# An encoder block with experts: the last iteration of the expert loop written out, and two weight loads moved between row tiles

## What is computed

```python
h = rms_norm(x, norm_mix)
x_in, b_g, c_g, q, k, v, gate_a, gate_b = split(h @ w_in)        # w_in: 1024 x 5120
y_conv = short_conv_mixer(x_in, b_g, c_g, conv_w) @ w_out_conv
y_attn = neighbourhood_attention(rms(q), rms(k), v, rpb) @ w_out_attn
x = x + (sigmoid(gate_a) * y_conv + sigmoid(gate_b) * y_attn) @ w_o
h = rms_norm(x, norm_ffn)
# experts: 32, of which each token goes to its top 4; rows of one expert are worked in blocks
g = minimum(xb @ w_gate[e] + b_gate[e], 7)
u = clip(xb @ w_up[e] + b_up[e], -7, 7)
act = g * sigmoid(1.702 * g) * (u + 1)
y_rows = (act @ w_down[e] + b_down[e]) * gate
x = x + segment_sum(y_rows, row_token)
```

## Time and profile before

| | us |
|---|---|
| median of 3 runs | 2313.76 |
| lowest and highest | 2313.57, 2314.39 |
| the profiled execution | 2312.18 |
| its span, first to last instruction | 2310.4 |
| its mean granted TensorE clock | 0.985 |
| busy: TensorE, its weight loads | 2225.3, 1563.2 |
| busy: VectorE, ScalarE, GpSimd | 1549.4, 1128.6, 879.5 |

### The profile page before, as it was taken

One profiled execution on the slowest core, in us unless ns is written; L12 is line 12 of the kernel. 1 busy time (PEld: TensorE's weight loads), 2 busy tenths in 40 slices (PEclk: granted clock), 3 DMA queues, 4 the chain that ended last, 5 costly groups with the idle time before them and its releaser, 6 DMA issues.

```text
span 2310.4 us, 35945 instructions
## 1 busy us (share of the span) xinstructions
PE 2225.3 (96%) x11550; PEld 1563.2 (68%) x11551; DVE 1549.4 (67%) x1953; ACT 1128.6 (49%) x1134; POOL 879.5 (38%) x494
## 2 busy tenths in 40 slices
PE   7999999999999869999999999999999999999995
PEld 5874554787888757776666667666676666666774
DVE  5544443444344588888777777787787777778884
ACT  4333223423231146766555556655565555556663
POOL 1242120000000036565444644565455534555562
PEclk9999999999999979999999999999999999999998
DMA  5422111232333369999888988898898888798994
GB/s 197 115 61 67 37 45 28 66 108 82 100 120 121 147 239 336 352 339 314 292 269 267 310 283 313 288 304 291 303 312 302 295 276 293 269 302 320 327 341 138
DMA packets 205432, 518.01 MB, mean 224 GB/s; under 512 B 18816, under 2 KB 85888, under 8 KB 205376
## 3 DMA queue, kind: packets, MB, share of 16 engines
q1 hardware_dynamic: 189248, 470.57, 56.7%
q0 software_dynamic: 16128, 46.67, 9.4%
HBM read 480.94 MB, written 32.05 MB: 222 GB/s over the span
## 4 chain that ended last, share of the span: by engine, by line
PE 77%; DVE 7%; DMA 6%; issue 5%; POOL 2%; ACT 2%; SPq 0%; DVEq 0%; ACTq 0%; POOLq 0%
PE psum L1751 13%; PE psum L1753 12%; PE psum L1752 12%; PE psum L1574 7%; DMA ring<-in_w_up 5%; PE psum L1762 5%; PE psum L1596 4%; PE psum L1595 4%; PE psum L1594 4%; DVE w_lo L1302 4%; PE psum L1804 3%; POOL rs L595 2%; PE psum L1680 1%; PE psum L1780 1%; PE psum L1681 1%
## 5 line engine op out<-in xcount | busy, mean ns | idle before, releaser
L1302 DVE TENSOR_TENSOR w_lo<-ring,w_hi 128x2048 fp32r<-128x2048 f32 x384 | 874.8, 2301 | 113.7 <-ACT w_hi L867 102.3
L867 ACT ACTIVATE w_hi<-ring 128x2048 fp32r<-128x2048 f32 x384 | 728.7, 1920 | 372.6 <-DMA ring<-in_w_up 249.4
L637 POOL TENSOR_SCALAR pick<-iota_bf,slot_col 128x256 bf16<-128x256 bf16 x252 | 487.1, 1946 | 148.3 <-DVE slot_col L1315 148.3
L1751 PE MATMUL psum<-w_hi,xT_hi 128*128 128x512 f32 x992 | 410.7, 414 | 20.5 <-DVE w_lo L1302 19.2
L1753 PE MATMUL psum<-w_hi,xT_lo 128*128 128x512 f32 x992 | 394.8, 398 | 0.0
L1752 PE MATMUL psum<-w_lo,xT_hi 128*128 128x512 f32 x992 | 394.0, 397 | 0.0
L1751 PEld LDWEIGHTS psum<-w_hi,xT_hi 128*128 128x128 f32 x992 | 187.3, 189 | 139.8 <-issue 57.7
L643 POOL DMA_INDIRECT xg<-h_rows,idx_new x33 | 73.9, 2240 | 512.5 <-DVE idx_new L1296 494.3
L1751 PE MATMUL psum<-w_hi,aT_hi 128*128 128x512 f32 x544 | 228.3, 420 | 9.4 <-issue 8.3
L1753 PEld LDWEIGHTS psum<-w_hi,xT_lo 128*128 128x128 f32 x992 | 187.8, 189 | 45.3
L1753 PE MATMUL psum<-w_hi,aT_lo 128*128 128x512 f32 x544 | 217.3, 399 | 0.0
(11 more groups left out here) (323 smaller groups left out, 3289.1 us busy)
## 6 DMA issues: line engine op xcount, KB each, us to landing
ring<-in_w_gate SPq DMA_DIRECT2D x256, 512.0 KB, 5.1
ring<-in_w_up SPq DMA_DIRECT2D x256, 512.0 KB, 6.5
ring<-in_w_down SPq DMA_DIRECT2D x256, 512.0 KB, 6.0
ring<-in_w_in SPq DMA_DIRECT2D x44, 512.0 KB, 5.1
ring<-in_x SPq DMA_DIRECT2D x16, 512.0 KB, 3.4
ring<-in_w_in SPq DMA_DIRECT2D x6, 1024.0 KB, 7.2
vb<-oT SPq DMA_DIRECT2D x16, 256.0 KB, 6.5
ring<-in_w_oc SPq DMA_DIRECT2D x16, 256.0 KB, 3.0
```

Source lines behind the costliest of these rows:

```text
L637: e.tensor_scalar(pick[:, t, :], iota_bf[:, :], slot_col[:, t, :], None, ALU.is_equal).then_inc(g_pick, 1)
L867: e.activation(w_hi[:, hs, :], ring[:, slot, :], ACT.Copy).then_inc(g_hi, 1)
L1302: e.tensor_tensor(w_lo[:, hs, :], ring[:, slot, :], w_hi[:, hs, :].bitcast(F32), ALU.subtract).then_inc(g_lo, 1)
L1751: e.matmul(dst, hi, w_up, start=start, stop=False)
```

## The change

**Front.** On SyncE the load of item 2 stands behind that of row tile 3, and that of item 3 behind row tile 4, each in the loop. On ScalarE the two `round_front` move from turns 3 and 4 to 5 and 6.

**Loop.** `table` now holds the passes less 2, so `n_loop` is 30, and each engine's last iteration is written out behind the loop, without the preparation of later passes. In it, VectorE does SwiGLU of the last pass between the third and the fourth chunk of the down of pass 30, and TensorE transposes it before the fourth chunk, into banks 0 and 1. The last pass's activations use the tiles `xT_hi`, `xT_lo` and `xTb`, since those of the activations are still read.

**Last down.** `last_down` does all chunks for the first half of the columns (bank 3, with the quarters in bank 2), then all for the second (bank 6). ScalarE scales `ysb` and the first half of `ys` after the first, the second half after the second. GpSimd scatters `ysb` after the first, `ys` after the second. ScalarE's copies of the last pass wait for `g_free` of the scatter of pass 30.

The diff, cut, engine by engine. SyncE:

```diff
             for t in range(2, TT):
                 e.wait_ge(xtr, t - 1)
                 e.dma_start(xt[t % 2], A["x"][P * t:P * t + P, :]).then_inc(x_in[t % 2], 16)
-            for n in range(2, 4):
-                load_item(n)
+                if 3 <= t < 5:
+                    load_item(t - 1)
...
+            with e.Fori(0, n_loop) as p:
+                loads_of_pass(p)
+            loads_of_pass(n_loop)
```

GpSimd:

```diff
-            scatter(n_loop)
-            scattered(n_loop)
-            e.sem_inc(g_free, 1)
-            scatter(n_loop + 1)
-            scattered(n_loop + 1)
+            for i in range(2):
+                scatter(n_loop + i)
+                scattered(n_loop + i)
+                e.sem_inc(g_free, 1)
+            hold(e, g_y, 2 * n_loop + 5)
+            e.indirect_dma_start(out=out_quarters, out_offset=bass.IndirectOffsetOnAxis(ap=idx_cur[:, 1:2], axis=0),
+                                 in_=ysb[:, :], in_offset=None, compute_op=ALU.add).then_inc(g_scb, 16)
+            hold(e, g_y, 2 * n_loop + 6)
+            e.indirect_dma_start(out=out, out_offset=bass.IndirectOffsetOnAxis(ap=idx_cur[:, 0:1], axis=0),
+                                 in_=ys[:, :], in_offset=None, compute_op=ALU.add).then_inc(g_sc, 16)
+            scattered(n_loop + 2)
```

ScalarE:

```diff
-                if t in (3, 4):
-                    round_front(t - 1)
+                if t in (5, 6):
+                    round_front(t - 3)
...
+            sigmoid(n_loop + 1, hbe)
+            for c in range(3, 6):
+                round_weights(n_loop, 16 + c, False)
+            act_rows(n_loop + 1, hbe, 0, 2, xT_hi, xTb)
+            round_weights(n_loop, 16 + 6, False)
+            y_out(n_loop + 1, hbm)
+            round_weights(n_loop, 16 + 7, False)
+            e.wait_ge(g_free, n_loop + 3)
+            e.wait_ge(g_shift, n_loop + 3)
+            hold(e, g_d, 2 * n_loop + 5)
+            with e.If(hbe > 0):
+                e.activation(ysb[:, :], bank[2][:, 0:QD], ACT.Copy, scale=gate_cur[:, 1:2])
+            e.activation(ys[:, 0:512], bank[3][:, :], ACT.Copy, scale=gate_cur[:, 0:1]).then_inc(g_y, 1)
+            e.wait_ge(g_d, 2 * n_loop + 6)
+            e.activation(ys[:, 512:D], bank[6][:, :], ACT.Copy, scale=gate_cur[:, 0:1]).then_inc(g_y, 1)
```

VectorE:

```diff
-            link(e.tensor_scalar(table[:, 2 * NT:], pinc[0:1, E - 1:E], -1.0, None, ALU.add))
+            link(e.tensor_scalar(table[:, 2 * NT:], pinc[0:1, E - 1:E], -2.0, None, ALU.add))
...
+            evacuate(n_loop + 1, hbe)
+            rest_of_weights(n_loop, 16 + 2)
+            swiglu(n_loop + 1, hbe)
+            rest_of_weights(n_loop, 16 + 3)
+            shift_rows(n_loop, False)
+            for c in range(4, 6):
+                rest_of_weights(n_loop, 16 + c)
+            rest_of_act(n_loop + 1, 0, xT_hi, xT_lo)
+            for c in range(6, 8):
+                rest_of_weights(n_loop, 16 + c)
+            shift_rows(n_loop + 1, True)
```

TensorE:

```diff
+            def last_act_transpose():
+                hold(e, g_act, n_loop + 2)
+                with e.If(hbe > 0):
+                    for i in range(2):
+                        e.transpose(bank[2][:, P * i:P * i + P], utb[:, P * i:P * i + P], ident[:, :])
+                for k in range(KT):
+                    ins = e.transpose(bank[k // 4][:, P * (k % 4):P * (k % 4) + P], ut[:, P * k:P * k + P], ident[:, :])
+                ins.then_inc(g_atr, 1)
...
+            def last_down(b):
+                for h in range(2):
+                    dst = bank[3 + 3 * h][:, :]
+                    for c in range(D_CHUNKS):
+                        at, slot, hs, _ = chunk_at(n_loop, 20 + c)
+                        if h == 0:
+                            e.wait_ge(g_lo, at + 1)
+                        for k in (2 * c, 2 * c + 1):
...
+                            product(dst, xT_hi[:, k, :], xT_lo[:, k, :], w_hi[:, hs, at0:at0 + 512], w_lo[:, hs, at0:at0 + 512], k == 0, False)
...
+                    e.matmul(dst, ones_bf[0:3, :], brow_d[:, 512 * h:512 * h + 512], start=False, stop=True).then_inc(g_d, 1)
...
+            with e.If(hbm < 1):
+                down_but_one(range(D_CHUNKS - 1), False)
+            last_act_transpose()
+            with e.If(hbm > 0):
+                down_but_one((D_CHUNKS - 1,), True)
+            with e.If(hbm < 1):
+                down_but_one((D_CHUNKS - 1,), False)
+            hold(e, g_alo, 2 * n_loop + 4)
+            with e.If(hbe > 0):
+                last_down(True)
+            with e.If(hbe < 1):
+                last_down(False)
```

More of the change, by code:

```diff
@@ L1887, in _ @@
                     down_all(False)
[L1888 to L1896 removed]
+            hbm = e.value_load(table[0:1, bass.ds(n_loop + NT, 1)], min_val=0, max_val=1)
```

113 lines of the change are left out of this document (72 added, 41 removed).

## The result

The changed kernel takes 2295.65 us (median of 4 runs, 2294.42 to 2297.44); the kernel before, timed beside it, 2314.07 (4 runs, 2313.57 to 2316.94). The ratio is 0.9918, with a 95% interval of 0.9901 to 0.9936: 18.4 us less. The case that I had called likeliest is nevertheless not the one that happened, as the traces show.

A forecast was written before the change was run, and what follows sets the result against it. TensorE was taken to bound the kernel (busy 2225.3 of 2310.4 us), clearly short at both ends and the routing. 2312.18 - 7.4 - 9.8 - 1.3 + 2.5 = 2296.2, with the median 1.6 higher: 2297.8 us, range 2294 to 2303.

The forecast's parts named there:

- The case that I had called likeliest: Behind the loop: one instruction-fetch stop at the first page of written-out code, giving 2297.8 us; chance 0.46.
- Part 1, the front: Start of the kernel: earlier key-weight loads and later roundings keep TensorE's transposes at 6.35 us a group; gain 7.4 us.
- Part 2, the work that goes: Last iteration written out: dropping the preparation of a pass never computed, costed at nothing, 0 to 1 us of gain.
- Part 2, the new order: Last two downs: last pass's activations prepared earlier, TensorE waits 2.9 us instead of 12.5; gain 9.8 us.
- Part 2, behind the last product: End of the kernel: first half's copy and quarter's scatter lie beside second half's products; gain 1.3 us (0.3 to 2.1).
- Part 3, the cold code: Behind the loop: one stop of 4.4 us for code run once, 1.9 given back, 2.5 us lost (bounds 0 and 8).
- the case with 0.24: Behind the loop: rival with no stop at all in the written-out code, 2295.3 us; chance 0.24.
- The second stop: At the last down: rival with a further stop at its branch, as long as the old one, 2302.2 us; chance 0.13.
- no row tile came late: Front: rival that a row tile or rounding becomes late, 3 to 7.4 us stay away, 2301 to 2305; chance 0.07.
- `ys` was free in time: End: rival that reused `ys` or VectorE's chain holds it up by 3 to 5 us, 2301 to 2303; chance 0.06.
- no branch of the written-out code cost a stop: Behind the loop: rival that each taken branch costs 4.4 us, seven on TensorE; chance 0.04 for four and more.

The follow-up runs named there:

- the mixed version: Changed kernel, VectorE's rest of the last activations behind the first weight chunk, only the last down's third and fourth chunks by halves: 2289.04 us, ratio 0.9902.

## Why the prediction was right, and where it was not

**Part 1, the front: right.** 7.4 us forecast; 7.45 in the transposes, 7.4 in the means at the first gate-up bias. The reading that the gain is TensorE's lost rhythm and not ScalarE's 10.1 us of waiting was the decisive one. I had priced the two edits as a pair; either does it alone.

**Part 2, the work that goes: a little short.** I costed the dead pass at 0 to 1 us, and took 0. The iteration ahead of the bias of pass 30 takes 39.7 to 40.2 us in the five traces with the old end and 37.8 to 39.2 in the nine with the new one (before and changed kernel: 40.16 and 38.79). Within it the waits for `w_lo` in the gate-up shrank to 0.32 us, from 0.70 and 0.32 in before. So this term is 1.4 us in these two traces.

**Part 2, the new order: right in its course, too good by 2.0 us.** The last pass's transposes, chunk and rest came where laid out: `xT_lo` ended 16.0 us behind the first product of the down of pass 30 (2250.05 to 2266.08), forecast 16.5. The end of the last bias was to come 16.65 us behind the start of that of pass 30 (26.45 less 9.8) and came after 18.65. The pause, 3.4 for 2.9, is 0.5 of it: between the last operand and the product stand 0.8 us, which I had taken as nothing. The clock is 1.0: I counted seven products at the lower clock, as before had them, and there were twelve; the shorter pause didn't bring fewer. The seven were one execution's number: the other traces of the old end have 11 to 14. Products and biases themselves are the last 0.5: with no wait and the clock at 1.00 they take 12.33 us (2263.45 to 2275.78 in the mixed version), where I added 11.2 and 0.6.

**Part 2, behind the last product: right.** 1.3 forecast (0.3 to 2.1), 1.05 by the two spans, 1.7 by undoing it.

**Part 3, the cold code: this step failed.** I forecast one stop at the first code behind the loop, 4.4 less 1.9 given back, 2.5 us lost, with 0.46. There was none; the case with 0.24 (2295.3) is what happened, and the time is 0.35 from it. That nearness is luck: the errors of the other terms, below, stand in that case too, and the same kernel, timed again, had a median of 2292.86, a little under the range of 2294 to 2303. What I got wrong is what the 4.4 us of before meant. I read the row as "code behind the loop is not there". The runs show that the stop belongs to the jump over the long body; that the jump lands beyond what is there is the reading that fits the packet ahead of the product. Code that is run through in order is fetched as it goes: the instruction queue has 41 packets for 37, and none of the four from 2228.5 to 2250.6 us stands at a wait for anything but `w_lo`, 0.32 us at most. My own evidence, the first iteration without a stop, spoke for this, and I gave it less weight than the row with the stop. The second stop, which I gave 0.13 for a jump as long as the one in before, can be had by a longer jump, as the doubled body shows, but not by this one.

**The sum.** Terms of the forecast: 7.4 + 9.8 + 1.3 - 2.5 = 16.0 us against the profiled execution. Measured: 7.98 + 0.87 + 7.80 + 1.05 = 17.7. The missing stop (2.5) and the lighter iteration (1.4) stand on one side, the 2.0 of the new order and 0.2 behind the last product on the other, and the front and the loop make up what is left. The remaining 0.4 to the medians is the step from the profiled execution to the median, 1.2 for 1.6. So the time was closer than its terms: 2.2 us, made of errors of up to 2.5 that partly cancel. The other rivals did not happen: no row tile came late, `ys` was free in time (ScalarE's first copy at 2275.65 was released by TensorE's bias), and no branch of the written-out code cost a stop.

## What to carry to other kernels

When an engine stands idle for a load, ask what is queued behind the waiting instruction. Moving the waiting work one step back and asking for the load earlier were each enough here, and the gain was the rhythm of the engine that both fed, not the length of the wait. Where a branch chooses between two bodies on a path that nothing covers, put the usual one first: the jump over the long one cost 3.9 us in the means at the end of before, and swapping them cost nothing here. Such a jump need not stop the engine, as the changed kernel shows. And write the last iteration of a software-pipelined loop out only with the order of each engine laid over the others, since what is late next (here VectorE's two chunks ahead of a rest that TensorE waits for) was worth another 3.4 to 4.6 us here, once the last down was mixed to fit it.

## What the hardware did that I had not expected

- Code that is only jumped over can cost time. Doubling a body that is never run added 3.5 us to the pause ahead of the next one, with one packet of 0.02 MB in the instruction queue ahead of the first product. In the changed kernel such a packet goes behind the first product, and nothing waits.
- Straight code behind a loop, run for the first time, cost nothing: the first product waited 0.15 or 0.16 us, for an operand, in all nine traces with the written-out iteration.
- A shorter pause does not mean fewer slow products. Behind 3.43 us of pause 12 products ran at the granted clock of 0.50 (1.2 GHz) in one trace of the changed kernel and 8 in the other; at the old end, with 12 us or more between bias and first product, it was seven in before and 12 with the front alone. Behind 1.23 us the clock stayed at 1.00 (2.4 GHz) and none did. What a shorter pause gives can so differ between executions by 1 us and more: in the means over the traces of the old end, taking away the stop shortened the pause by 3.9 and the stretch to the last bias by 3.3.
